# Causal mask and position bias: from matrix products into the row maximum, in a kernel of two transformer blocks

## The reference

```python
# block 1, "fox": 8 heads of 64; c is the running sum of log f
logits = q @ k.T * scale + c[:, None] - c[None, :]
logits = where(kpos <= qpos, logits, -inf);  p = softmax(logits)
# block 1, "diff": 4 heads, two score matrices each
logits_m = where(kpos <= qpos, q_m @ k_m.T * scale, -inf)
p = softmax(logits_1) - lam * softmax(logits_2)
# block 2, "moba": 8 heads of 64, a learned bias for each head and bucket of distance
s = q @ k.T * scale + table[bucket(qpos - kpos), head]
s = where(qpos - kpos >= 0, s, -inf);  p = softmax(s)
```

## Time and profile before

| | us |
|---|---|
| runs (3) | 1194.89, 1194.90, 1195.82; median 1194.9 |
| span of the profiled execution | 1194.0 |
| PE busy | 1178.5 |
| PEld busy | 984.1 |
| DVE busy | 742.4 |
| ACT busy | 623.6 |
| POOL busy | 158.6 |

### The profile page before, as it was taken

The page is one execution under the profiler, slowest core; times in us unless marked ns, Lnnn a source line. Parts: engine busy times, 40 slices in busy tenths (PEclk is TensorE's granted clock), DMA queues, the critical chain, the costliest instruction groups (busy, mean ns, idle before and its releaser), DMA issues.

```text
span 1194.0 us, 16132 instructions
## 1 busy us (share of the span) xinstructions
PE 1178.5 (99%) x6034; PEld 984.1 (82%) x6034; DVE 742.4 (62%) x1123; ACT 623.6 (52%) x1054; POOL 158.6 (13%) x255
## 2 busy tenths in 40 slices
PE   9999999999999999999999999999999999999997
PEld 7788887778888888888788898888898888888886
DVE  6667576755333475674387775455647659558478
ACT  5566785685332255532676554352455445464464
POOL 3233223410000021000133000010001010000010
PEclk9999999999999999999999999999999999999999
DMA  6422233113443543342112545221286553743732
GB/s 198 108 58 66 71 91 103 37 54 106 106 105 105 176 132 102 106 142 71 36 54 106 162 139 165 71 101 51 73 247 141 172 130 87 227 108 91 210 71 88
DMA packets 152139, 133.37 MB, mean 112 GB/s; under 512 B 5553, under 2 KB 124401, under 8 KB 152066
## 3 DMA queue, kind: packets, MB, share of 16 engines
q1 hardware_dynamic: 144688, 113.13, 31.6%
q0 software_dynamic: 4000, 13.67, 5.9%
q10 hardware_dynamic: 3378, 5.60, 1.5%
HBM read 115.55 MB, written 4.22 MB: 100 GB/s over the span
## 4 chain that ended last, share of the span: by engine, by line
PE 90%; DVE 5%; ACT 2%; DMA 1%; issue 1%; POOL 0%; DVEq 0%; ACTq 0%; POOLq 0%
PE lin L993 23%; PE lin L995 23%; PE lin L994 23%; PE tr L1175 2%; PE sc L994 2%; PE sc L995 2%; PE sc L993 2%; PE sc L1189 1%; PE sc L1185 1%; PE tr L1168 1%; PE tr L994 1%; PE tr L993 1%; PE tr L995 1%; DVE w_lo L2368 1%; PE lin L1213 1%
## 5 line engine op out<-in xcount | busy, mean ns | idle before, releaser
L993 PE MATMUL lin<-h_hi,w_hi 128*128 128x512 f32 (+1 forms) x824 | 318.0, 386 | 0.0
L995 PE MATMUL lin<-h_hi,w_lo 128*128 128x512 f32 (+1 forms) x824 | 310.5, 377 | 0.0
L994 PE MATMUL lin<-h_lo,w_hi 128*128 128x512 f32 (+1 forms) x824 | 310.4, 377 | 0.0
L2368 DVE TENSOR_TENSOR w_lo<-w_raw,w_hi 128x1024 fp32r<-128x1024 f32 x160 | 196.6, 1232 | 140.8 <-ACT w_hi L1637 139.7
L1637 ACT ACTIVATE w_hi<-w_raw 128x1024 fp32r<-128x1024 f32 x162 | 170.8, 1056 | 145.0 <-PE lin L995 48.6
L995 PEld LDWEIGHTS lin<-h_hi,w_lo 128*128 128x128 f32 x824 | 155.7, 189 | 28.5
L993 PEld LDWEIGHTS lin<-h_hi,w_hi 128*128 128x128 f32 x824 | 155.8, 189 | 27.2 <-issue 0.6
L994 PEld LDWEIGHTS lin<-h_lo,w_hi 128*128 128x128 f32 x824 | 156.1, 189 | 24.5
L2393 DVE TENSOR_REDUCE neg_max<-sc 128x1 f32<-128x128 f32 (+3 forms) x112 | 52.4, 478 | 55.4 <-PE sc L1189 35.5
L2368 DVE TENSOR_TENSOR u_lo<-u_raw,u_hi 128x256 fp32r<-128x256 f32 (+2 forms) x48 | 37.4, 779 | 68.6 <-ACT u_hi L2252 37.4
L993 PE MATMUL lin<-w_hi,h_hi 128*128 128x512 f32 x160 | 63.4, 397 | 0.0
(11 more groups left out here) (399 smaller groups left out, 2356.6 us busy)
## 6 DMA issues: line engine op xcount, KB each, us to landing
w_raw<-in_w_in SPq DMA_DIRECT2D x74, 512.0 KB, 3.9
w_raw<-in_w_up SPq DMA_DIRECT2D x32, 512.0 KB, 4.4
wd_b<-in_w_down SPq DMA_DIRECT2D x24, 512.0 KB, 5.3
w_raw<-in_w_out SPq DMA_DIRECT2D x16, 512.0 KB, 3.6
w_raw<-in_w_xkv SPq DMA_DIRECT2D x16, 512.0 KB, 3.9
x_m<-in_x SPq DMA_DIRECT2D x8, 512.0 KB, 5.6
w_raw<-in_w_branch SPq DMA_DIRECT2D x8, 512.0 KB, 4.2
w_raw<-in_w_xq SPq DMA_DIRECT2D x8, 512.0 KB, 3.9
```

The source lines that it names most:

```text
L993: pe.matmul(o, lh, rh, start=start, stop=False)
L994: pe.matmul(o, lh, rl, start=False, stop=False)
L995: return pe.matmul(o, ll, rh, start=False, stop=stop)
L2368: return dve.tensor_tensor(out, x, as_f32(hi), ALU.subtract)
```

## The change

Mask and bias no longer enter the scores as products. VectorE adds a tile to the scores in the operation that finds the row maximum, writes the negated sum to `p0` (or `px`), and ScalarE takes the exponential there in place, with scale -1. The bank `sc` is released by the maximum. The wait for the transposes that read `p0` last moves from ScalarE to VectorE.

```diff
 def stacked_scores(s, place, h, i, q_rest=None):
     if s >= 2:
-        pe.wait_ge(s_exp, s - 1)
+        pe.wait_ge(s_max, s - 1)
...
     pe.matmul(o, q, keys(place, h)[:, 0:n], start=True, stop=False)
-    extra(o, n)
...
-def mask(o, i):
-    pe.matmul(o[:, P * i:P * i + P], ident_b[:, :], future_b[:, :], start=False, stop=False)
...
-    def extra(o, n):
-        for tile in (bias_16[h], bias_16[8 + h]):
-            pe.matmul(o[:, P * near:n], flip[:, :], tile[:, 256 - (n - P * near):256],
-                      start=False, stop=False)
...
-def exponentials(s, p, n):
+def exponentials(s, p, x, sign):
     act.wait_ge(s_max, s + 1)
-    act.activation(p, sc[:, s % 2, 0:n], ACT.Exp, bias=neg_max[:, s:s + 1],
+    act.activation(p, x, ACT.Exp, bias=neg_max[:, s:s + 1], scale=sign,
                    accum_out=denom[:, s:s + 1]).then_inc(s_exp, 1)
...
+def biased_max(s, p, bias):
+    dve.wait_ge(s_done, s + 1)
+    n = p.shape[1]
+    dve.tensor_tensor_reduce(p, sc[:, s % 2, 0:n], bias[:, T - n:T], -1.0, 3.0e38, ALU.add, ALU.min,
+                             neg_max[:, s:s + 1]).then_inc(s_max, 1)
...
+def causal_max(name, bias):
+    def f(m):
+        if m >= 4:
+            dve.wait_ge(tr_done, R0[name] + m - 3)
+        biased_max(S0[name] + m, probs_of(B["p0"], m % 4), bias(m // 4))
+    return f
```

```diff
+BIAS_ROW = 640
...
 def bias_rows():
...
-    dve.tensor_scalar(B["beta"][0:8, :], lin[0:8, g % 4, 0:BIAS_COLS], B["beta_0"][0:8, 0:1], None,
-                      ALU.subtract).then_inc(dve_evac, 1)
+    dve.memset(B["beta"][0:8, 0:far], 0.0)
+    dve.tensor_scalar(B["beta"][0:8, far:BIAS_ROW], lin[0:8, g % 4, 0:BIAS_COLS], B["beta_0"][0:8, 0:1],
+                      None, ALU.subtract).then_inc(dve_evac, 1)
     dve.wait_ge(dve_evac, DN[g])
-    link(dve.memset(B["beta"][0:8, 257:BIAS_COLS], FAR))
-    link(dve.tensor_copy(B["beta_hi"][0:8, :], B["beta"][0:8, :]))
-    lo_part(B["beta_lo"][0:8, :], B["beta"][0:8, :], B["beta_hi"][0:8, :]).then_inc(beta_ready, 1)
+    dve.memset(B["beta"][0:8, far + 257:BIAS_ROW], FAR).then_inc(beta_ready, 1)
...
 def bias_rows_out():
     act.wait_ge(beta_ready, 1)
-    act.dma_start(bias_dram[0:8, :], as_f32(B["beta_hi"][0:8, :])).then_inc(beta_out, 16)
-    act.dma_start(bias_dram[8:16, :], as_f32(B["beta_lo"][0:8, :])).then_inc(beta_out, 16)
+    rows = B["beta"][0:8, :].rearrange("p (o r) -> p o r", o=1).to_broadcast([8, P, BIAS_ROW])
+    act.dma_start(bias_dram[:, :, :], rows).then_inc(beta_out, 16)
...
-    src = bass.AP(bias_dram.tensor, first * BIAS_COLS + 1, [[1, P], [BIAS_COLS, n], [1, 256]])
+    src = bass.AP(bias_dram.tensor, first * P * BIAS_ROW + P,
+                  [[BIAS_ROW - 1, P], [P * BIAS_ROW, n], [1, T]])
...
-tensors["bias_dram"] = nc.dram_tensor("bias_dram", (16, BIAS_COLS), F32, kind="Internal").ap()
+tensors["bias_dram"] = nc.dram_tensor("bias_dram", (8, P, BIAS_ROW), F32, kind="Internal").ap()
```

More of the change, by code:

```diff
@@ L822, in _ @@
             pool.wait_ge(ones_made, 1)
-            for buf, value in ((ident[:, :], 0.0), (as_f32(ones_r[:, :]), 1.0), (as_f32(flip[:, :]), 0.0), (ident_b[:, :], 0.0),
-                               (future_b[:, :], 0.0), (minus_half[:, :], -0.5),
+            for buf, value in ((ident[:, :], 0.0), (as_f32(ones_r[:, :]), 1.0), (minus_half[:, :], -0.5),
                                (eps_n[:, 0:1], SUBLN_EPS), (eps_n[:, 1:2], EPS)):
                 link(pool.memset(buf, value))
[L827 to L830, removed]
+            pool.affine_select(out=ident[:, :], in_=ident[:, :], compare_op=ALU.not_equal, fill=1.0, base=0,
                                pattern=[[-1, P]], channel_multiplier=1).then_inc(consts_made, 1)
@@ L834, in _ @@
                 root(N0["norm1"] + t)
+            pool.memset(bias_c[:, :], 0.0).then_inc(mask_cleared, 1)
+            pool.wait_ge(mask_cleared, 1)
+            own_block = bias_c[:, T - P:T]
+            pool.affine_select(out=own_block, in_=own_block, compare_op=ALU.is_ge, fill=FAR, base=0,
+                               pattern=[[-1, P]], channel_multiplier=1).then_inc(mask_made, 1)
+            pool.wait_ge(mask_made, 1)
             emptied = [0]
@@ L1266, in _ @@
             hh, hl = B["h_hi"], B["h_lo"]
+            warm = ones[:, :].bitcast(BF16)[:, 0:P]
             for n in range(2 * WARM):
-                pe.matmul(lin[:, 3, 0:P], ident_b[:, :], future_b[:, :], start=True, stop=True)
+                pe.matmul(lin[:, 3, 0:P], warm, warm, start=True, stop=True)
             for t in range(2):
@@ L1352, in diff_scores @@
                 for m in range(2):
-                    stacked_scores(S0["diff"] + 2 * w + m, 1, 2 * h + m, i, lambda o, n: mask(o, i))
+                    stacked_scores(S0["diff"] + 2 * w + m, 1, 2 * h + m, i)
             def diff_turn(w):
@@ L1993, in bias_rows_out @@
                 act.wait_ge(beta_ready, 1)
-                act.dma_start(bias_dram[0:8, :], as_f32(B["beta_hi"][0:8, :])).then_inc(beta_out, 16)
-                act.dma_start(bias_dram[8:16, :], as_f32(B["beta_lo"][0:8, :])).then_inc(beta_out, 16)
+                rows = B["beta"][0:8, :].rearrange("p (o r) -> p o r", o=1).to_broadcast([8, P, BIAS_ROW])
+                act.dma_start(bias_dram[:, :, :], rows).then_inc(beta_out, 16)
             def bias_tiles_in():
[L1998 to L2002, removed]
-                        src = bass.AP(bias_dram.tensor, first * BIAS_COLS + 1, [[1, P], [BIAS_COLS, n], [1, 256]])
-                        act.dma_start(as_f32(place).rearrange("p (h c) -> p h c", h=n), src).then_inc(bias_in, 16)
-                        first += n
+                act.wait_ge(beta_out, 16)
+                first = 0
+                for place in bias_places:
+                    n = place.shape[1] // T
+                    src = bass.AP(bias_dram.tensor, first * P * BIAS_ROW + P,
+                                  [[BIAS_ROW - 1, P], [P * BIAS_ROW, n], [1, T]])
+                    act.dma_start(place.rearrange("p (h c) -> p h c", h=n), src).then_inc(bias_in, 16)
+                    first += n
             step(G["glr"][0])
```

70 lines of the change are left out of this document (34 added, 36 removed).

## The result

The changed kernel takes 1220.3 us (median of 4 runs, 1219.2 to 1221.1) where the kernel before takes 1195.4 beside it: a ratio of 1.021, 95% interval 1.0196 to 1.0224. The forecast was 1210 with a range of 1191 to 1221, so the measured time lies at its very end. Two things happened at once, as in the prediction: the three attention stages became shorter, and TensorE stood still in front of gla. The standing was 8.7 us longer than forecast.

A forecast was written before the change was run, and what follows sets the result against it. TensorE's matrix work was taken to bound most of the kernel, VectorE part of the third stage. 1194.9 less 10.9 gained in the stages plus 26.2 lost before the third gave 1210.2, forecast 1210 us, range 1191 to 1221.

The forecast's parts named there:

- the write's rate: Bias write to DRAM before the third stage: 2.62 MB from eight partitions at 61 GB/s, 43 us, ending near 513.
- Mechanism (a): Before the third stage: weight halves take turns with the write, TensorE loses 24.5 us, 26.2 with the clock; 1210, chance 0.50.
- The clock: After TensorE's idle stretch before the third stage: a lower granted clock over 6 us costs 1.7 us.
- (b): Before the third stage: weights pass freely, only the wait for the write's end holds, 17.5 us lost; 1201, chance 0.22.
- 25.3 us: Weight half issued at 476.7 behind the write: 3.8 us plus 64 turns of 0.336, landing at 502.0.
- Rival (c): Before the third stage: the write is quick, 150 GB/s, landing at 488 before ScalarE needs it; 1184, chance 0.15.
- Rival (d): Attention stages: VectorE's new row-maximum operation runs at half speed, 0.33 us more each, 32 us of VectorE; 1223, chance 0.08.
- The stages: All three attention stages: removed mask and bias products, less VectorE's added work, gain 10.9 us together.
- First: First attention stage: TensorE stays the bound, 32 masks of 0.11 us removed, 3.5 us gained.
- Second: Second attention stage: TensorE 36.1 and VectorE 36.2 us, neither hiding the other fully; 38.5 instead of 43, 4.5 gained.
- Third: Third attention stage: 1.2 gained before 596 us, 1.3 lost from 596 to 620, 3.0 gained behind; 2.9 in all.
- That can only help the second stage: Score bank released by the row maximum, not the exponential: frees some of the second stage's 3.4 us without TensorE work.

The follow-up runs named there:

- Run 1: The kernel before with the large bias write from eight partitions added, masks, bias products and its own small writes kept: 1230.5 us, ratio 1.030.
- run 2: The changed kernel with 64 copies of each bias row written instead of 128, half the bytes: 1197.0 us, ratio 1.002 to the kernel before.
- run 8: The changed kernel with ScalarE's four value copies moved ahead of the conversions of late weight halves: 1216.9 us, ratio 1.018 to the kernel before.
- run 3: The changed kernel with the same bias bytes written from 128 partitions instead of eight neighbours: 1184.4 us, ratio 0.991 to the kernel before.
- 9: The changed kernel with the bias written from eight partitions four apart (0, 4 to 28): 1183.9 us, ratio 0.991 to the kernel before.
- run 11: The kernel of run 3 with 64 products of zeros put back, one per tile of the first two stages: 1188.8 us, ratio 0.995 to the kernel before.
- 12: The kernel of run 3 timed again, unchanged, with more rounds: 1183.5 us, ratio 0.990 to the kernel before.
- runs 9 to 12: 9, run 11, 12, and one more: the kernel of run 3 with the score bank released by the exponential again, 1187.0 us, ratio 0.993.

## Why the prediction was right, and where its sizes were off

**The step that was off: the write's rate.** "I take 43, the row nearest in place and direction": it took 51.6, and 43 had been the longest of the three values that the rows gave. Everything behind it is this term. The product restarted 3.9 us behind the write's end in the forecast (512.7 and 516.6) and 3.3 in the run (515.3 and 518.6). The gap was 33.2 instead of 24.5, 8.7 more, and the write was 8.6 longer.

The row was the right one, but its rate was read too high. "12.3 KB in 0.2 us, 61 GB/s" comes from slices of 0.1 us, three of which hold the bytes. The same small write in a window of its own size, 469.76 to 470.00 us of the kernel before (8 pieces of 1,536 B, and 6 of 4 B):
```profile
DMA packets 14, 0.01 MB, mean 51 GB/s; under 512 B 6, under 2 KB 14, under 8 KB 14
```
That is the rate of the large write, and 2.62 MB at 51 GB/s are 51 us. The Trainium skill's rule on ports ("SBUF — State Buffer", section on the DMA port swizzle) gave 48 us and stood nearer than 43. The time stayed inside the range by less than 1 us: its upper end had been made for a write 5 us longer together with smaller gains, not for one 8.6 us longer.

**Mechanism (a).** Right in its place (gap from 485.4, forecast near 485), its chain (half of `ka2`, value copy, bank, product) and its eight engines. The clock cost about 2.0, forecast 1.7. Run 1 puts the loss on the write, run 2 sets the semaphore (b) aside, run 8 confirms ScalarE's order as a small part. "25.3 us" from issue to landing for the first half was wrong, 41.6: ahead of the 64 turns it lost some 15 us in which the write's engines served no weights. The time did not feel it, because the next half had to wait for the end of the write in either case.

**Rival (c), the quick write,** was wrong for eight neighbouring partitions. Its time, 1184.0, came true in runs 3 and 9 (1184.4 and 1183.9). **Rival (d)** is out: 487 ns median, no pass over 0.7 us.

**The stages.** 10.7 gained, forecast 10.9: the sum is better than its parts, and that is luck. First: 3.9 for 3.5; a mask was worth 0.11 us, as taken. Second: 2.8 for 4.5. "Neither can hide the other fully" was the case, and more so: TensorE stands 4.8 us for `pt_lo`, and putting 32 products back costs 1.9 us there (run 11) where 3.5 was taken. Third: 4.0 for 2.9. When the 17th of its 32 tiles starts (620.7 before, 647.1 after), 2.1 of it is there, where the forecast had 0.1 lost; behind it come 1.9 where 3.0 was taken. The accumulator's read took 0.083 us, not 0.13; whether that is what made the difference, no run shows. "That can only help the second stage" was wrong: of the early release's gain the second stage has 1.8, the third 0.8, the first 0.6. The exponential from SBUF takes 36 ns more (560 for 524 median) and hides, as taken.

**The version to keep** is that of runs 3 and 12, or 9: the change with its write from a better place, 0.990 (0.9886 to 0.9917) of the kernel before. The three are one result. In the profiled executions the granted clock dips once between 455 and 467 us in the kernel before, the changed kernel and run 3 (0.72 to 0.76 over 6 us) and stays 1.00 in runs 9 to 12; that is some 1.5 us which no edit here explains. Reading one copy of each row with partitions stepping backwards, which would need no copies at all, was not tried.

## What to carry to other kernels

A transfer is priced by where its bytes lie as well as by how many they are: before copying a few rows many times, count the partitions and groups of four that they come from, and spread the rows when they are made. Spreading wider is not spreading better: every fourth partition gave 209 GB/s, every sixteenth 99. A slow transfer also costs the queues beside it: look at what shares its engines, and at the first instruction that waits for that, before asking who waits for the transfer itself. And read the rate of a short transfer in a window of its own length: coarse slices made 61 GB/s of 51 here, and that was most of the forecast's error.

## What the runs showed of the hardware

Eight rows from neighbouring partitions leave at 51 GB/s, from every fourth at 209, though both hold eight engines. Two queues on one engine alternated piece by piece whatever the size (399 pieces for 399 with 2,560 B, 234 for 234 with 1,280 B), so a queue of 512 B pieces beside one of 2,560 B gets a sixth of the bytes. Ahead of the turns lay 14 to 15 us in which the later queue got almost nothing on those engines. That stretch did not halve with the pieces or with the length of the write, and was some 8 us beside a write of twice the rate. Its cause stays open.
